# Two transformer blocks in fp32 on one core: weight block sums of the seven-product down projection made on GpSimd

## Chip, cores and metric

One core of one Trainium2 chip runs the whole program. The metric is the device time in microseconds (us). The kernel before was run twice: 1784.21 and 1784.86 us, median 1784.53 us.

## What is computed

Two blocks follow one another on 512 rows of 1024 values: the first holds windowed attention, a gated recurrence and a mixture of experts; the second holds a feed forward layer, a mixer and another feed forward layer. The change lies in the two feed forward layers of the second block.

```python
def swiglu_ffn(x, w_gate, w_up, w_down):
    return (jax.nn.silu(x @ w_gate) * (x @ w_up)) @ w_down

def second_block(x, ...):
    for l in range(DEPTH):
        x = x + 0.5 * swiglu_ffn(rmsnorm(x, ffn1_norm[l]), ffn1_w_gate[l], ffn1_w_up[l], ffn1_w_down[l])
        x = x + hybrid_mixer(rmsnorm(x, mix_norm[l]), w_in[l], ...)
        x = x + 0.5 * swiglu_ffn(rmsnorm(x, ffn2_norm[l]), ffn2_w_gate[l], ffn2_w_up[l], ffn2_w_down[l])
        x = rmsnorm(x, final_norm[l])
    return x
```

The inner width `D_FF` is 2816, and everything is float32.

## The kernel before

Every large product is made of three fp32r products. A weight block of 128x2048 values ("unit") is loaded by a DMA of SyncE's queue into one of four buffers `raw`. ScalarE rounds it into `hi` (`rounded`, line 1862), VectorE makes the rest `lo = raw - hi` (`rest`, line 2271), and TensorE multiplies hi by the high part of the left side, lo by the high part, and hi by the low part. There are two pairs of hi and lo, used in turn: `rounded` of a unit waits until the product that used the pair two units earlier is done. TensorE waits for a unit's hi and lo before its first matmul.

The inner width is worked in three parts (`FPARTS`): 1024, 1024 and 768 columns. For each part come the gate and up products (`mm`, lines 1557 to 1559: a unit serves four blocks of 128 rows, 48 matmuls), then that part's share of the down product. For the first two parts this share is made by a seven-product scheme (a 2 by 2 block product with seven block products in place of eight). `make_plan_ffn` and `schedule_seven` set it out. The down weights of the part are four blocks b11, b21, b12, b22. Four sums of them are made first:

- T3 = b22 - b12, written over b12
- T2 = T3 + b11, written into a buffer of its own, `XW`
- T4 = b21 - T2, written over b21
- T1 = b22 - T2, written over b11

The seven products (`seven`, lines 1526 to 1528, 24 matmuls each) run in this order of weight units: b11, b21, T2, T3, T4, then half of the next part's first gate product, T1, the other half, b22. Their left sides are blocks of the hidden values and sums of them (S1 to S4, A22), whose low parts VectorE makes in `sum_lo` (line 2345). `seven_x` (line 2378) adds each result from PSUM to `x_sb` on VectorE.

So the scheme runs at four places of the program: twice in the first feed forward layer (about 960 and 1085 us) and twice in the second (about 1492 and 1617 us). I call them the four places, and the products by their position, first to seventh.

The order of the work on each engine is one list of steps, written out by hand (`schedule_ffn`, `schedule_seven`); each engine walks the list and does its own kinds of step, in the list's order, and waits on semaphores for the others. In this list T3 and T2 stand inside the up product before the scheme, T4 behind the second product's steps, T1 behind the results of the second and fourth product. The loads stand in the order b12, b22, b11, b21, and each waits until its buffer has been rounded and subtracted (`raw_free`).

GpSimd issues a few small DMAs and makes one addition (line 1364, for the mixer's bias) in this half of the program.

```python
SEVEN = ("P1", "P2", "P6", "P7", "P4", "P5", "P3")
...
            b12, b22 = units(key, wd, r // 128, r // 128 + 8, 512, 1024)
            t1, t2, t4 = (Unit(key, None, 4, 512) for _ in range(3))
...
            plan.extend([b11, b21, t2, b12, t4, g0, t1, g1, b22])
            loads.extend([b12, b22, b11, b21, g0, g1])
```

Of the kernel before, what the change touches and what calls it, by code (L numbers as in the profile page):

```python
# [5 lines left out]
ALU = mybir.AluOpType  # L6
# [845 lines left out]
def program(nc, I, out):  # L852
# [15 lines left out]
    with ctx:  # L868
        sigs = []

        def sig(name, by=1):
            s = Sig(ctx.enter_context(nc.semaphore(name)), by)
            sigs.append(s)
            return s
# [22 lines left out]
        def cst(n):  # L897
            o, w = CW[n]
            return C1[:, o:o + w]

        def bc(a, axis, shape):
            return a.unsqueeze(axis).broadcast_to(shape)
# [141 lines left out]
        d_w = [sig(f"d_w{i}", 16) for i in range(NU)]  # L1044
# [5 lines left out]
        a_hi, v_lo = sig("a_rounded"), sig("v_rest")  # L1050
        p_mm, a_ev, v_ev = sig("p_product"), sig("a_evicted"), sig("v_evicted")
        p_at, a_at, v_at = sig("p_attn"), sig("a_attn"), sig("v_attn")
        p_hg, a_hg, v_hg, g_hg = sig("p_hgrn"), sig("a_hgrn"), sig("v_hgrn"), sig("g_hgrn")
        p_rt, a_rt, v_rt, g_rt = sig("p_route"), sig("a_route"), sig("v_route"), sig("g_route")
        a_sum, v_sum, v_made = sig("a_sum"), sig("v_sum"), sig("v_made")
        p_m2, a_m2, v_m2, g_m2 = sig("p_mix2"), sig("a_mix2"), sig("v_mix2"), sig("g_mix2")

        class Moe:
# [9 lines left out]
        U = p1 + p2 + p3 + p4 + p5  # L1068
# [4 lines left out]
        def split_events(u):  # L1073
            return [(a_hi, u), (v_lo, u)]

        made = {}
# [4 lines left out]
        def blocks(n, p):  # L1081

            return [U.index(q) for q in U if q.key == (n, "s", p)]

        def raw_done(q):

            n, _, p = q.key if q.key[1:2] == ("s",) else (None, None, None)
            u = U.index(q)
            if n and u == blocks(n, p)[0]:
                return split_events(made[n, p, "T1"])  # L1090
            if n and u == blocks(n, p)[1]:
                return split_events(made[n, p, "T4"])
            return split_events(u)

        def place_ffn(first, n, loads, at_raw, at_hl, own=()):
# [81 lines left out]
        n = next(j for j, q in enumerate(experts) if q[:3] == ("gu", "g", NP - 3))  # L1177
        experts, experts_tail = experts[:n], experts[n:]
        experts_tail.insert(1 + next(j for j, q in enumerate(experts_tail) if q[:2] == ("turn_h", NP - 1)), ("table",))
        n, done = schedule_opening(joint, feed3, experts_tail)  # L1180
# [3 lines left out]
        n = after.index(("mm", ("ffn1", "u", 0, 0), 0, 1, first3 + 2))  # L1184
# [138 lines left out]
        def pool_program(pool):  # L1323
            e = pool.e
            def z_load(c):
                pool.wait_ge(d_z[0], (10, 14)[c])
                pool.wait_ge(d_z[1], (11, 15)[c])
                if c == 0:
                    pool.wait_ge(p_mm, (("zb1",), 1, 3))
                else:  # L1330
                    pool.wait_ge(v_hg, ("hTl", 3))
                for w in range(2):
                    e.dma_start(zw[c][w][:, :, :], zsp[8 * w + 4 * c:8 * w + 4 * c + 4, :, :].rearrange("i p n -> p i n")).then_inc(*d_zr[2 * c + w](c))

            def r_load():
                pool.wait_ge(v_hg, ("hTl", 3))
                e.dma_start(n2p[:, :], I["norm2_w"].rearrange("o (p k) -> p (o k)", k=8)).then_inc(*d_r(0))
                e.dma_start(WR[:, :, :], I["w_router"]).then_inc(*d_r(1))
                e.dma_start(BR[:, :], I["b_router"].partition_broadcast(128)[:, 0, :]).then_inc(*d_r(2))

            todo = {"z_load": z_load, "r_load": r_load}
            for name, *a in before + experts:
                if name in todo:
                    todo[name](*a)
            yield None, {}

            def row(name):
                e.dma_start(rows[name][:, :], I[{"ffn1": "ffn1_norm_2", "n2": "mix_norm_2", "ffn2": "ffn2_norm_2"}[name]].partition_broadcast(
                    128)[:, 0, :]).then_inc(*d_row[name](0))

            pool.wait_ge(main.p, ("cols", NP // GP - 1, 7))
            row("ffn1")
            pool.wait_ge(p_mm, (("ffn1", "g", 0, 0), 1, 3))
            row("n2")
            for w, name in enumerate(("q_norm_2", "k_norm_2")):
                for h in range(2):
                    e.dma_start(qkw[64 * h:64 * h + 64, w:w + 1], I[name].rearrange("o d -> d o")).then_inc(*d_b((w, h)))
            e.dma_start(PW[:, :, :], I["pool_w_2"][0].rearrange("g c d -> c g d")).then_inc(*d_b("pool"))

            def m2_bias():  # L1360
                pool.wait_ge(v_norm, ("n2", "l", 3, 1))
                e.dma_start(Bt[:, :, :], I["rel_tile"]).then_inc(*d_bt(0))
                pool.wait_ge(d_bt, 0)
                e.tensor_tensor(Bt[:, :, 128:256], Bt[:, :, 128:256], bc(cst("cmask"), 1, [128, 8, 128]),
                                ALU.add).then_inc(*g_m2("bias"))
                pool.wait_ge(v_ev, (("ffn1", "d", 2, 1), 3))
                e.memset(up[:, :, 0:16], 0.0).then_inc(*g_m2("up0"))

            def m2_row():
                pool.wait_ge(v_m2, ("dd", 3))  # L1370
                row("ffn2")

            todo = {"m2_bias": m2_bias, "m2_row": m2_row}
            for name, *a in after:
                if name in todo:
                    todo[name](*a)
# [472 lines left out]
        def act_program(act):  # L1849
            e = act.e  # L1850

            def rounded(u, part=None):
                q = U[u]
                w = q.kc * q.n
                a, b = ((0, w) if part is None else (part * w // 2, part * w // 2 + w // 2))
                if q.made:
                    act.wait_ge(v_made, (q.made, q.key[0], q.key[2]))
                else:
                    act.wait_ge(d_w[q.slot], u)
                for s, k in q.hl_free:  # L1860
                    act.wait_ge(s, k)
                e.copy(q.hi[:, a:b], q.raw[:, a:b]).then_inc(*a_hi((u, 0) if part == 0 else u))  # L1862
# [250 lines left out]
            def route():  # L2113
# [5 lines left out]
            todo = {"warm": warm_up, "norm": norm, "turned": turned, "rope": rope, "bounds": bounds, "ev": ev, "at_square": at_square, "at_qT": at_qT,  # L2119
                    "at_kT": at_kT, "at_scores": at_scores, "at_turn": at_turn, "at_values": at_values,  # L2120
                    "hg_log": hg_log, "hg_k": hg_k, "z_sig": z_sig, "hg_table": hg_table, "hg_decay": hg_decay, "hg_tail1": hg_tail1, "at_high": at_high,
                    "hg_tail3": hg_tail3, "hg_out": hg_out, "hg_var": hg_var, "hg_turn": hg_turn, "hn": norm_hn,
                    "hn_turn": hn_turn, "hn_half": hn_half, "hnh": hn_high, "route": route}
# [136 lines left out]
        def dve_program(dve):  # L2260
            e = dve.e
# [77 lines left out]
            def sum_lo(n, p, w):  # L2339
# [3 lines left out]
                else:  # L2343
                    dve.wait_ge(a_sum, (w, n, p))
                e.tensor_tensor(l[:, :, :], v, h.bitcast(F32) if w == "A22" else h[:, :, :].bitcast(F32),
                                ALU.subtract).then_inc(*v_sum((w + "l", n, p)))

            def made_(n, p, w):
                b11, b21, t2, b12, t4, t1, b22 = (U[u].raw[:, :] for u in blocks(n, p))
                u11, u21, _, u12, _, u1, u22 = blocks(n, p)  # L2350
                done = v_made((w, n, p))
                if w == "T3":
                    dve.wait_ge(d_w[U[u12].slot], u12)
                    dve.wait_ge(d_w[U[u22].slot], u22)
                    e.tensor_tensor(b12, b22, b12, ALU.subtract).then_inc(*done)
                elif w == "T2":
                    dve.wait_ge(d_w[U[u11].slot], u11)
                    dve.wait_ge(v_made, ("T3", n, p))
                    if p:
                        dve.wait_ge(v_lo, made[n, p - 1, "T2"])  # L2360
                        dve.wait_ge(v_made, ("T1", n, p - 1))
                    e.tensor_tensor(t2, b12, b11, ALU.add).then_inc(*done)
                elif w == "T1":
                    dve.wait_ge(v_lo, u11)
                    dve.wait_ge(v_made, ("T2", n, p))
                    e.tensor_tensor(t1, b22, t2, ALU.subtract).then_inc(*done)
                else:
                    dve.wait_ge(v_lo, u21)
                    dve.wait_ge(v_made, ("T2", n, p))
                    e.tensor_tensor(t4, b21, t2, ALU.subtract).then_inc(*done)  # L2370

            def seven_x(n, p, pr, t):
                r, c = QUARTER[pr]
# [542 lines left out]
            def wo2(tb, c, half):  # L2916
                if half:
# [1 line left out]
                    dve.wait_ge(p_m2, ("wo2", tb, c, 1))  # L2919
                    e.tensor_tensor(v, v, PS[:, c, :], ALU.add).then_inc(*v_m2(("x", tb, c)))  # L2920

            todo = {"sum": sum_, "sum_lo": sum_lo, "made": made_, "seven_x": seven_x, "half": half, "normed": normed, "turned": turned, "turn_hidden": turn_hidden, "ev": ev, "m2_norm": m2_norm, "m2_pool": m2_pool, "m2_scores": m2_scores, "m2_weights": m2_weights,
                    "m2_values": m2_values, "m2_pooled": m2_pooled, "wo2": wo2, "lo": todo["lo"]}
            for name, *a in after:
                if name in todo:
# [170 lines left out]
```

## Time and profile before

| | us |
|---|---|
| the two runs, median | 1784.53 |
| span of the profiled execution | 1785.5 |
| TensorE busy | 1748.2 |
| VectorE busy | 923.1 |
| ScalarE busy | 603.3 |
| GpSimd busy | 12.5 |

The profiled execution is known by its span, 1785.5 us; no separate device time is given for it. The span lies 1.0 us above the median of the runs.

PE is TensorE's matmuls, PEld its weight loads (one goes ahead of each matmul), DVE VectorE, ACT ScalarE, POOL GpSimd, SPq SyncE's DMA queue. In a row of instructions stand the start, the duration, the engine, the line of the kernel, the operation, what it writes and reads, and in brackets how long the engine was idle before it and who released it. Matmuls are pipelined: each is shown as some 390 ns long while one starts every 227 ns.

### The profile page before, as it was taken

The numbers are of one execution on the slowest core, as the hardware profiler recorded it, in microseconds if no ns is written. First come the engines' busy times: TensorE is split into PE (matmuls) and PEld (weight loads), VectorE is DVE, ScalarE is ACT, GpSimd is POOL, SyncE is SP. The second block draws the span as 40 slices with busy tenths as digits, with TensorE's granted clock in tenths as the row PEclk, the third lists the DMA queues.
The fourth block names the chain that finished last, engine by engine and source line by source line (L and its number), as shares of the span: only waits on it lengthen the run. The fifth ranks groups of instructions, "written<-read, shape, count | busy, mean of one in ns | idle before, by whom it ended". The sixth has DMA issues, their size and how long they took to land.

```text
span 1785.5 us, 20614 instructions
## 1 busy us (share of the span) xinstructions
PE 1748.2 (98%) x8607; PEld 1284.3 (72%) x8607; DVE 923.1 (52%) x1339; ACT 603.3 (34%) x938; POOL 12.5 (1%) x22
## 2 busy tenths in 40 slices
PE   7999999998999999999999999999999999999998
PEld 6878888875454544544478888888877888888886
DVE  5768865643333333333444745635578535736634
ACT  4556335442111111111233323324355433423322
POOL 0000000000000000000000000000000000000000
PEclk9999999998999999999999999999999999999999
DMA  6222225547999999999832242233321232241331
GB/s 219 90 71 72 95 83 177 192 161 288 422 421 421 421 421 421 420 421 421 340 114 71 72 141 71 91 122 98 115 71 37 80 133 71 71 159 54 108 104 59
DMA packets 93315, 331.16 MB, mean 185 GB/s; under 512 B 6192, under 2 KB 15552, under 8 KB 68512
## 3 DMA queue, kind: packets, MB, share of 16 engines
q1 hardware_dynamic: 88928, 318.33, 46.8%
q0 software_dynamic: 1984, 7.25, 1.2%
q10 hardware_dynamic: 2304, 4.20, 0.6%
q8 instruction: 70, 1.15, 0.3%
q14 instruction: 29, 0.24, 0.0%
HBM read 323.46 MB, written 6.29 MB: 185 GB/s over the span
## 4 chain that ended last, share of the span: by engine, by line
PE 91%; DVE 5%; ACT 3%; DMA 0%; issue 0%; SPq 0%; DVEq 0%; ACTq 0%
PE PS L1427 12%; PE PS L1557 11%; PE PS L1559 10%; PE PS L1558 10%; PE PS L1460 6%; PE PS L1553 5%; PE PS L1555 5%; PE PS L1554 5%; PE PS L1527 3%; PE PS L1528 3%; PE PS L1526 3%; PE PS L1398 2%; PE PS L1470 2%; PE PS L1399 2%; PE PS L1631 2%; PE PS L1471 2%
## 5 line engine op out<-in xcount | busy, mean ns | idle before, releaser
L2271 DVE TENSOR_TENSOR lo<-raw,hi 128x1024 fp32r<-128x1024 f32 (+2 forms) x147 | 250.4, 1709 | 318.7 <-ACT hi L1862 315.5
L1862 ACT CAST hi<-raw 128x1024 fp32r<-128x1024 f32 (+2 forms) x149 | 214.2, 1446 | 297.9 <-PE PS L1559 111.9
L1557 PE MATMUL PS<-xh_ffn,hi 128*128 128x512 f32 x576 | 225.0, 391 | 0.0
L1559 PE MATMUL PS<-xh_ffn,lo 128*128 128x512 f32 x576 | 224.3, 389 | 0.0
L1558 PE MATMUL PS<-xl_ffn,hi 128*128 128x512 f32 x576 | 224.2, 389 | 0.0
L1559 PEld LDWEIGHTS PS<-xh_ffn,lo 128*128 128x128 f32 x576 | 108.1, 188 | 22.6
L1558 PEld LDWEIGHTS PS<-xl_ffn,hi 128*128 128x128 f32 x576 | 108.2, 188 | 22.2
L1557 PEld LDWEIGHTS PS<-xh_ffn,hi 128*128 128x128 f32 x576 | 108.2, 188 | 22.2
L1427 PE MATMUL PS<-raw,XG 128*64 128x512 f32 x352 | 117.1, 593 | 0.0
L2231 DVE TENSOR_TENSOR HF<-SG,PS 128x512 f32<-128x512 f32 x16 | 17.4, 1090 | 165.0 <-PE PS L1427 165.0
L2246 DVE SCALAR_TENSOR_TENSOR YL<-PS,SM,YH 128x512 fp32r<-128x512 f32 x30 | 21.1, 746 | 138.8 <-ACT YH L1845 138.8
L2254 DVE TENSOR_TENSOR x_sb<-x_sb,PS 128x512 f32<-128x512 f32 x128 | 78.2, 677 | 8.7 <-PE PS L1471 8.7
L1557 PE MATMUL PS<-xTh,hi 128*128 128x512 f32 x192 | 78.3, 408 | 0.5 <-DVE lo L2271 0.3
L1427 PE MATMUL PS<-rawz,XG 128*64 128x512 f32 x280 | 77.7, 592 | 0.0
L1559 PE MATMUL PS<-xTh,lo 128*128 128x512 f32 x192 | 75.0, 391 | 0.0
L1558 PE MATMUL PS<-xTl,hi 128*128 128x512 f32 x192 | 75.0, 391 | 0.0
L1427 PEld LDWEIGHTS PS<-raw,XG 128*64 128x64 f32 x352 | 36.4, 137 | 49.6 <-issue 49.5
L1828 ACT COPY HT<-PS 128x512 f32<-128x512 f32 x16 | 9.4, 586 | 175.1 <-PE PS L1436 175.1
L1398 PE MATMUL PS<-SE,hnh 128*128 128x256 f32 x256 | 65.4, 294 | 0.2 <-DVE SE L2204 0.2
L1399 PE MATMUL PS<-SE,hnl 128*128 128x256 f32 x256 | 63.7, 288 | 0.0
L1427 PEld LDWEIGHTS PS<-rawz,XG 128*64 128x64 f32 x280 | 24.8, 137 | 38.8 <-issue 38.8
L1845 ACT ACTIVATE YH<-PS,SM 128x512 fp32r<-128x512 f32 x30 | 19.0, 683 | 99.8 <-PE PS L1460 99.8
(510 smaller groups left out, 3678.3 us busy)
## 6 DMA issues: line engine op xcount, KB each, us to landing
raw<-in_w_in SPq DMA_DIRECT2D x26, 1024.0 KB, 5.2
rawz<-in_w_down_experts SPq DMA_DIRECT2D x25, 1024.0 KB, 10.1
raw<-in_w_up_experts SPq DMA_DIRECT2D x24, 1024.0 KB, 14.8
raw<-in_w_gate_experts SPq DMA_DIRECT2D x20, 1024.0 KB, 15.0
raw<-in_ffn_w_down SPq DMA_DIRECT2D x20, 1024.0 KB, 5.0
rawz<-in_w_up_experts SPq DMA_DIRECT2D x19, 1024.0 KB, 18.8
raw<-in_w_down_experts SPq DMA_DIRECT2D x16, 1024.0 KB, 11.5
rawz<-in_w_gate_experts SPq DMA_DIRECT2D x16, 1024.0 KB, 13.1
```

The costliest lines, as they stand in the source:

```text
L1398: e.matmul(PS[:, b, 0:GP * 128], hnh[:, tb, f], sv, start=tb == 0, stop=False)
L1399: x = e.matmul(PS[:, b, 0:GP * 128], hnl[:, tb, f], sv, start=False, stop=tb == 3)
L1427: x = e.matmul(PS[64 * q:64 * q + 64, b, :], XG[(i // GP) % 2][:, k, s:s + 64], w[q][:, kk * 512:kk * 512 + 512], start=k == 0, stop=k == 7)
L1460: x = e.matmul(PS[64 * q:64 * q + 64, b + c, :], HT[:, j, 64 * q:64 * q + 64], w[q][:, jj * D + c * 512:jj * D + c * 512 + 512], start=j = ...
L1553: e.matmul(o, xh[:, k, c], h[:, kk, :], start=s0, stop=False)
L1554: e.matmul(o, xh[:, k, c], l[:, kk, :], start=False, stop=False)
L1555: x = e.matmul(o, xl[:, k, c], h[:, kk, :], start=False, stop=s1)
L1557: e.matmul(o, h[:, kk, c], xh[:, k, :], start=s0, stop=False)
L1558: e.matmul(o, h[:, kk, c], xl[:, k, :], start=False, stop=False)
L1559: x = e.matmul(o, l[:, kk, c], xh[:, k, :], start=False, stop=s1)
L1862: e.copy(q.hi[:, a:b], q.raw[:, a:b]).then_inc(*a_hi((u, 0) if part == 0 else u))
L2271: e.tensor_tensor(q.lo[:, a:b], q.raw[:, a:b], q.hi[:, a:b].bitcast(F32), ALU.subtract).then_inc(*v_lo(key))
```

## The change

The four sums of blocks are made by GpSimd, with the same operations and operands. They signal `g_made` in place of `v_made`. Waits that VectorE's own order made needless are written out: T2 waits for the up product's first eviction (its buffer XW is in use before), and the buffer of T3 is reloaded only after T2 has read it. Nothing else on any engine is changed.

```diff
@@ raw_done, inside program
                 return split_events(made[n, p, "T4"])
+            if q.made == "T3":
+                return split_events(u) + [(g_made, ("T2", n, p))]
             return split_events(u)
@@ pool_program
-            todo = {"m2_bias": m2_bias, "m2_row": m2_row}
+            def made_(n, p, w):
+                b11, b21, t2, b12, t4, t1, b22 = (U[u].raw[:, :] for u in blocks(n, p))
+                u11, u21, _, u12, _, u1, u22 = blocks(n, p)
+                done = g_made((w, n, p))
+                if w == "T3":
+                    pool.wait_ge(d_w[U[u12].slot], u12)
+                    pool.wait_ge(d_w[U[u22].slot], u22)
+                    e.tensor_tensor(b12, b22, b12, ALU.subtract).then_inc(*done)
+                elif w == "T2":
+                    pool.wait_ge(d_w[U[u11].slot], u11)
+                    pool.wait_ge(g_made, ("T3", n, p))
+                    if p:
+                        pool.wait_ge(v_lo, made[n, p - 1, "T2"])
+                        pool.wait_ge(g_made, ("T1", n, p - 1))
+                    else:
+                        pool.wait_ge(v_ev, ((n, "u", 0, 0), 3))
+                    e.tensor_tensor(t2, b12, b11, ALU.add).then_inc(*done)
+                elif w == "T1":
+                    pool.wait_ge(v_lo, u11)
+                    pool.wait_ge(g_made, ("T2", n, p))
+                    e.tensor_tensor(t1, b22, t2, ALU.subtract).then_inc(*done)
+                else:
+                    pool.wait_ge(v_lo, u21)
+                    pool.wait_ge(g_made, ("T2", n, p))
+                    e.tensor_tensor(t4, b21, t2, ALU.subtract).then_inc(*done)
+
+            todo = {"m2_bias": m2_bias, "m2_row": m2_row, "made": made_}
@@ rounded, in act_program
-                    act.wait_ge(v_made, (q.made, q.key[0], q.key[2]))
+                    act.wait_ge(g_made, (q.made, q.key[0], q.key[2]))
@@ dve_program
-            def made_(n, p, w):
...
```

VectorE's instructions at the first place, from the rest of b21 (raw_52) to the rest of T4, before. XW is T2, raw_49 holds T3, raw_51 b11 and raw_50 b22:

```order
L2271 TENSOR_TENSOR lo_56<-raw_52,hi_54 128x1024 [waits a_rounded] x2
L2345 TENSOR_TENSOR S2l<-hA,S2h 128x1024 [waits a_sum]
L2378 SCALAR_TENSOR_TENSOR x_sb<-PS,x_sb 128x512 [waits p_product] x2
L2271 TENSOR_TENSOR lo_55<-XW,hi_53 128x2048 [waits a_rounded]
L2370 TENSOR_TENSOR raw_52<-raw_52,XW 128x2048 [waits v_made,v_rest]
L2271 TENSOR_TENSOR lo_56<-raw_49,hi_54 128x2048 [waits a_rounded]
```

The same stretch of VectorE after the change:

```order
L2299 TENSOR_TENSOR lo_56<-raw_52,hi_54 128x1024 [waits a_rounded] x2
L2373 TENSOR_TENSOR S2l<-hA,S2h 128x1024 [waits a_sum]
L2382 SCALAR_TENSOR_TENSOR x_sb<-PS,x_sb 128x512 [waits p_product] x2
L2299 TENSOR_TENSOR lo_55<-XW,hi_53 128x2048 [waits a_rounded]
L2299 TENSOR_TENSOR lo_56<-raw_49,hi_54 128x2048 [waits a_rounded]
```

T4 is gone from between the rests of T2 and T3; T1, which stood eight rows further on, is gone as well. GpSimd's instructions between its small DMAs and the mixer's bias, after the change (before, the bias DMA of line 1362 followed the small DMAs at once):

```order
L1382 TENSOR_TENSOR raw_49<-raw_50,raw_49 128x2048 [waits d_w4,d_w3]
L1391 TENSOR_TENSOR XW<-raw_49,raw_51 128x2048 [waits v_evicted,g_made,d_w5]
L1399 TENSOR_TENSOR raw_52<-raw_52,XW 128x2048 [waits g_made,v_rest]
L1395 TENSOR_TENSOR raw_51<-raw_50,XW 128x2048
L1382 TENSOR_TENSOR raw_49<-raw_52,raw_49 128x2048 [waits d_w0,d_w3]
```

These are T3, T2, T4 and T1 of the first place, then T3 of the second. T3 waits for its two loads alone, T4 for the rest of b21, and T1 has no wait left: it stands directly behind T4.

## Rows read from the trace of the kernel before

**Rows 1.** The page: span, busy time, chain that ended last.

```profile
span 1785.5 us, 20614 instructions
...
PE 1748.2 (98%) x8607; PEld 1284.3 (72%) x8607; DVE 923.1 (52%) x1339; ACT 603.3 (34%) x938; POOL 12.5 (1%) x22
...
PE 91%; DVE 5%; ACT 3%; DMA 0%; issue 0%; SPq 0%; DVEq 0%; ACTq 0%
```

**Rows 2.** Four places by stage: stretch, length, busy by engine, PEclk, DMA, GB/s.

```profile
960.00:1030.00 70.00, 70.00 (x311) 57.99 (x310) 50.43 (x48) 25.23 (x20) 0.00 (x0) 1.00 0.20 64
1085.00:1155.00 70.00, 70.00 (x310) 58.00 (x309) 51.17 (x48) 25.10 (x21) 0.00 (x0) 1.00 0.16 51
1492.00:1562.00 70.00, 70.00 (x311) 57.96 (x310) 50.16 (x48) 25.50 (x20) 0.00 (x0) 1.00 0.20 65
1617.00:1687.00 70.00, 70.00 (x310) 57.98 (x309) 51.23 (x49) 25.36 (x21) 0.00 (x0) 1.00 0.16 52
```

**Rows 3.** Lines 2355, 2362, 2366: duration ns min/median/max, first and last start us.

```profile
L2355 DVE TENSOR_TENSOR raw<-raw,raw x4: 2282/2283/2284, 967.0 to 1624.3; 128x2048 f32<-128x2048 f32 x4
...
L2362 DVE TENSOR_TENSOR XW<-raw,raw x4: 2292/2292/2294, 969.3 to 1626.7; 128x2048 f32<-128x2048 f32 x4
...
L2366 DVE TENSOR_TENSOR raw<-raw,XW x4: 2282/2283/2284, 1010.0 to 1666.7; 128x2048 f32<-128x2048 f32 x4
```

**Rows 4.** Timeline, VectorE, first place: start, duration, instruction, idle before.

```profile
986.40 2.36 DVE L2271 TENSOR_TENSOR lo<-raw,hi 128x1024 fp32r<-128x1024 f32 x2 [0.39 <-ACT hi L1862]
988.68 1.22 DVE L2345 TENSOR_TENSOR S2l<-hA,S2h 128x1024 fp32r<-128x1024 f32 x1
989.82 1.28 DVE L2378 SCALAR_TENSOR_TENSOR x_sb<-PS,x_sb 128x512 f32<-128x512 f32 x2
991.80 2.29 DVE L2271 TENSOR_TENSOR lo<-XW,hi 128x2048 fp32r<-128x2048 f32 x1 [0.70 <-ACT hi L1862]
994.01 2.28 DVE L2370 TENSOR_TENSOR raw<-raw,XW 128x2048 f32<-128x2048 f32 x1
996.91 2.29 DVE L2271 TENSOR_TENSOR lo<-raw,hi 128x2048 fp32r<-128x2048 f32 x1 [0.62 <-ACT hi L1862]
```

**Rows 5.** Line 1526, weight loads: the third, fourth, sixth product; the second place's third.

```profile
L1526 PEld LDWEIGHTS PS<-hi,S2h x8: 188/188/188, 994.5 to 999.3; 128*128 128x128 f32 x8
...
L1526 PEld LDWEIGHTS PS<-hi,S3h x8: 187/188/188, 1000.0 to 1004.7; 128*128 128x128 f32 x8
...
L1526 PEld LDWEIGHTS PS<-hi,S1h x8: 187/188/188, 1021.7 to 1026.5; 128*128 128x128 f32 x8
...
L1526 PEld LDWEIGHTS PS<-hi,S2h x8: 187/188/188, 1119.7 to 1124.4; 128*128 128x128 f32 x8
```

**Rows 6.** Timeline of ScalarE, the roundings at the first place.

```profile
962.81 1.90 ACT L1862 CAST hi<-raw 128x2048 fp32r<-128x2048 f32 x1
973.25 1.91 ACT L1862 CAST hi<-raw 128x2048 fp32r<-128x2048 f32 x1 [8.54 <-PE PS L1559]
...
989.85 1.92 ACT L1862 CAST hi<-XW 128x2048 fp32r<-128x2048 f32 x1 [1.59 <-PE PS L1528]
994.96 1.92 ACT L1862 CAST hi<-raw 128x2048 fp32r<-128x2048 f32 x1 [3.19 <-PE PS L1528]
...
1012.37 1.91 ACT L1862 CAST hi<-raw 128x2048 fp32r<-128x2048 f32 x1 [3.61 <-DVE raw L2366]
```

**Rows 7.** GpSimd's one addition, and VectorE's next instruction after it.

```profile
1266.27 2.40 POOL L1364 TENSOR_TENSOR Bt<-Bt,C 128x1024 f32<-128x1024 f32 x1 [4.67 <-DMA Bt<-in_rel_tile]
...
1269.46 2.29 DVE L2271 TENSOR_TENSOR lo<-raw,hi 128x2048 fp32r<-128x2048 f32 x1 [6.75 <-ACT hi L1862]
```

**Rows 8.** Loads of b22 and b11 as issued, and the loads' time to landing.

```profile
942.97 0.37 SPq L1274 DMA_DIRECT2D raw<-in_ffn_w_down  x1
...
956.18 0.37 SPq L1274 DMA_DIRECT2D raw<-in_ffn_w_down  x1
...
raw<-in_ffn_w_down SPq DMA_DIRECT2D x4, 1024.0 KB, 5.0
```

More of the change, by code:

```diff
@@ L1054, in program @@
         p_rt, a_rt, v_rt, g_rt = sig("p_route"), sig("a_route"), sig("v_route"), sig("g_route")
-        a_sum, v_sum, v_made = sig("a_sum"), sig("v_sum"), sig("v_made")
+        a_sum, v_sum, g_made = sig("a_sum"), sig("v_sum"), sig("g_made")
         p_m2, a_m2, v_m2, g_m2 = sig("p_mix2"), sig("a_mix2"), sig("v_mix2"), sig("g_mix2")
@@ L2346, in sum_lo @@
                                 ALU.subtract).then_inc(*v_sum((w + "l", n, p)))
-            def made_(n, p, w):
[L2349 to L2370, printed above, removed]
             def seven_x(n, p, pr, t):
@@ L2920, in wo2 @@
                     e.tensor_tensor(v, v, PS[:, c, :], ALU.add).then_inc(*v_m2(("x", tb, c)))
-            todo = {"sum": sum_, "sum_lo": sum_lo, "made": made_, "seven_x": seven_x, "half": half, "normed": normed, "turned": turned, "turn_hidden": turn_hidden, "ev": ev, "m2_norm": m2_norm, "m2_pool": m2_pool, "m2_scores": m2_scores, "m2_weights": m2_weights,
+            todo = {"sum": sum_, "sum_lo": sum_lo, "seven_x": seven_x, "half": half, "normed": normed, "turned": turned, "turn_hidden": turn_hidden, "ev": ev, "m2_norm": m2_norm, "m2_pool": m2_pool, "m2_scores": m2_scores, "m2_weights": m2_weights,
                     "m2_values": m2_values, "m2_pooled": m2_pooled, "wo2": wo2, "lo": todo["lo"]}
```

## The prediction

> **What bounds the kernel now.** I read the page first. TensorE is busy for 1748.2 of 1785.5 us and carries 91% of the chain that ended last; VectorE has half its time free and GpSimd nearly all of it [rows 1]. A share over the whole span says little of one stage, so I then cut the four places of the change out, 70 us each. In every one the matmuls fill 70.00 of 70.00 us at full granted clock, while VectorE is busy for 50 to 51 us and ScalarE for 25 [rows 2]. TensorE never waits there. So nothing that VectorE is spared at these places can shorten the program: its removed time was already hidden. What can change is the other sign. A unit's rest (lo) must be ready before its product starts, and how much time it has to spare decides whether a disturbance is seen.
>
> I read that spare time from the timeline of VectorE at the first place against the weight loads of the products. The rest of T2 starts at 991.80 and takes 2.29 us, so it ends at 994.1 [rows 4]; the third product's first weight load is at 994.5 [rows 5]. 0.4 us to spare. The rest of T3 ends at 996.91 + 2.29 = 999.2, and the fourth product starts at 1000.0: 0.8 us. The reason for so little is that there are only two hi/lo pairs: the rounding of T2 starts when the first product is done (989.85, released by TensorE), the rounding of T3 when the second is (994.96) [rows 6], and one product takes about 5.4 us, while rounding and rest take 1.9 + 2.3 = 4.2. At the second place the third product starts at 1119.7 [rows 5], 125.2 later than at the first, and the pattern is the same; the third and fourth place repeat them.
>
> **The change, part by part.**
>
> *Removed from VectorE:* 16 subtractions and additions of 128x2048, 2.28 to 2.29 us each [rows 3], 36.6 us in all. VectorE falls to about 886 us. Gain on the path: none, by the full TensorE of rows 2. T1 shows this well. ScalarE waits 3.61 us for it before it rounds at 1012.37 [rows 6], which looks like a cost, but the sixth product starts only at 1021.7 [rows 5]. That wait goes and nothing is gained: what ends last there is TensorE's own queue.
>
> *Added to GpSimd:* the same 16 operations. The only two-input operation of GpSimd in the trace is the bias addition, 2.40 us for 1024 elements a partition, with VectorE idle all the while (its next instruction starts at 1269.46) [rows 7]. VectorE takes 1.22 us for 1024 [rows 4] and 2.28 for 2048, so 0.16 us of an operation is fixed. For 2048 elements on GpSimd the bounds are 2.3 us, if it were as quick as VectorE at that length, and 4.8 us, twice the row. I take 4.7, just under twice the row since some part will be fixed as on VectorE. GpSimd's busy time rises from 12.5 to some 88 us. The Trainium skill (GPSIMD Engine Reference, Performance versus the Vector engine) gives 4.5 us for this operation and 2.29 for VectorE's; rows 3 agree with the second, and rows 7 with a ratio of about two.
>
> *T3 and T2.* T3 now needs only its loads. b22 is issued at 942.97 and lands 5.0 later [rows 8], so T3 runs at 948.0 to 952.7. b11 is issued at 956.18, so T2 runs at 961.2 to 965.9. It is wanted at 989.85 [rows 6]: 24 us to spare. Cost nothing, even if GpSimd's first operation starts some microseconds late. If T2 disturbs the rest of an up unit, that costs nothing either: two roundings are there 10.4 us apart (962.81 and 973.25) [rows 6], and rounding, a whole GpSimd operation and the rest take 1.9 + 4.7 + 2.3 = 8.9.
>
> *T4 and T1, as results.* T4 may start when the rest of b21 ends, 986.40 + 2.36 = 988.8 [rows 4], and its rounding waits for the third product's end, about 1000.4 (one product of 5.4 behind 994.96). T1 stands directly behind T4 on GpSimd with no wait of its own, and is wanted at about 1011. Alone they would be done at 993.5 and 998.2. On time.
>
> *T4 and T1, as neighbours.* Here is the cost. Before, no two-input operation ran on both engines at once. Now T4 and T1 fill some 9.4 us just when the rests of T2 and T3, with 0.4 and 0.8 us to spare, must run. No row shows the two engines reading together, so I bound it: below by nothing (they do not disturb each other; a gain is excluded by the full TensorE), above by one operation waiting for the whole of the other. I take the upper end in its plain form, in which the engine that has waited goes first. GpSimd needs 2.34 ns for an element against VectorE's 1.2 [rows 7, 4], as an engine does that fetches its two inputs one after another over one way, so I expect that way to be full and not to leave room for a partner. This is a choice, not a reading.
>
> Step by step: S2l holds until 988.68 + 1.22 = 989.9 [rows 4]. T4 runs 989.9 to 994.6. The additions to x_sb have one input in PSUM and go on. The rest of T2, ready to start at 991.80, waits until 994.6 and ends at 996.9: the third product starts 2.4 us late (994.5 to 996.9). T1 has waited longest and runs 996.9 to 1001.6; the rest of T3 runs 1001.6 to 1003.9, where the fourth product was due at 1000.0 + 2.4 = 1002.4: 1.5 more. Then GpSimd is done, and the rest of T4 has only its usual neighbours. Together 3.9 us a place; with D for the GpSimd operation this is 2D - 5.5. TensorE is full behind, so nothing gives it back. Four places: 4 x 3.9 = 15.6 us, a span of 1785.5 + 15.6 = 1801.1; the span is 1.0 above the median of the runs, so 1784.5 + 15.6 = 1800.1 us, or 0.9% slower.
>
> The Trainium skill speaks against this change (SBUF — State Buffer, Who interferes with whom): a VectorE instruction with both inputs in SBUF fetches the second through the read interface that GpSimd uses, and the same section tells of a lock on the shared ports held for a whole instruction, whoever starts first. By this rule of the Trainium skill, with the 4.5 us of its GPSIMD Engine Reference, the place costs 2 x 4.5 - 5.5 = 3.5 us and the time is 1798.5. The trace of the kernel before neither shows nor denies it.
>
> *The written-out waits:* the wait of T2 for the up eviction is long over, and the reload of T3's buffer waits anyway for T3's own rest, 30 us after T2. Nothing. GpSimd's later work (the bias at 1266 [rows 7]) stands 130 us behind T1 of the second place. Nothing.
>
> **Rivals.**
>
> *The two engines do not disturb each other (not slower).* Then the removed time was hidden, the added time is hidden, and the time stays at 1784.5. For it: nothing in the trace speaks of interference, and one product's spare time is untouched. Against it: only that the operations are of the kind that might share. It decides if the rest of T2 still takes 2.3 us beside T4. A stretch of it by up to 0.4 us is free too.
>
> *They share.* Both slow down while they overlap. An operation of VectorE may then stretch between not at all and, with the whole of GpSimd's 4.7 us added, three times; at some 1.6 times the rest of T2 takes 3.7 us, ends at about 995.5 (S2l before it ends 0.7 later, still in time) and costs 1.0 to 1.1; the rest of T3 ends at 1000.5, in time for 1001.1. 4 x 1.1 = 4.4: 1789 us.
>
> *GpSimd keeps its turn.* T1 has no wait, so it may follow T4 before VectorE gets in. Then the rest of T2 ends at 989.9 + 9.4 + 2.3 = 1001.6, 7.1 late; the rest of T3 ends at 1003.9, before 1007.1. 4 x 7.1 = 28.4: 1812.9 us. It would be slower by over 2% (8.9 us a place) if an operation took over 5.6 us, since the place costs 2D - 2.3.
>
> **How the numbers follow.** Whole operations wait, in turn: 0.47 (1795 to 1801 as one or both rests wait; 1800.1 is the point). Share: 0.20. No disturbance: 0.20. GpSimd keeps its turn: 0.10, of which a third with operations slow enough to pass 2%. Rest 0.03. The range runs from 1783.8, to hold the case without disturbance with the spread of the runs (0.65 us), to 1808, which leaves out the case of the kept turn. A measurement tells about 2% (36 us) from no change: faster 0.01, within 2% 0.95, slower by more 0.04.
>
> **What would show each step.** The profile after should have 16 additions on GpSimd, 4.5 to 4.8 us long where undisturbed; T3 at 948 and T2 at 961; T4 within 1 us of the end of S2l, T1 right behind it or behind one VectorE operation. The waiting shows as a rest of T2 that starts or ends 2 to 3 us late, be it as idle time or as a duration of 5 us, and as waits of line 1526 for line 2299, twice a place, 2.4 and 1.5 us. TensorE busy in the four stretches would fall from 70 to about 66. I am wrong if those rests keep 2.3 us (no disturbance), if they stretch to 3 to 4 us (sharing), or if TensorE waits somewhere else, above all at T3 or T2.

## The result, and the profile after

The changed kernel took 1800.95 and 1803.22 us, median 1802.09, against 1784.53 before: 1.0095 times as long, 95% interval 1.0078 to 1.0112. Forecast were 1800.1 us and a range of 1783.8 to 1808.0. The ratios and intervals here and below are those recorded with the runs; they differ from the quotients of the medians (here 1.0098) by up to 0.0004. The profiled execution's device time was 1800.95 us, its span 1798.8. Measured again in five runs on one chip with the kernel before (e1_after), the ratio is 1.0083 (1.0070 to 1.0097). The cost is well under the 2% that the prediction took as the least that a measurement can tell, and still clear of the scatter.

The page of the kernel after, answering to [rows 1]:

```profile
span 1798.8 us, 20614 instructions
...
PE 1748.6 (97%) x8607; PEld 1281.7 (71%) x8607; DVE 925.9 (51%) x1323; ACT 603.5 (34%) x938; POOL 98.0 (5%) x38
...
PE 89%; DVE 6%; ACT 4%; issue 0%; DMA 0%; SPq 0%; DVEq 0%; ACTq 0%
```

TensorE does the same work in a span 13.3 us longer. The odd number is VectorE's: it lost 36.6 us of work and is shown busier than before, 925.9 against 923.1. So something else is counted as its busy time, and the waiting is not to be looked for under idle time alone.

The four places, by stage, answering to [rows 2]:

```profile
960.00:1030.00 70.00, 66.73 (x294) 54.66 (x293) 48.47 (x43) 23.66 (x19) 16.00 (x3) 1.00 0.19 61
1085.00:1155.00 70.00, 66.73 (x294) 54.65 (x293) 50.56 (x44) 23.78 (x20) 16.76 (x3) 1.00 0.20 64
1492.00:1562.00 70.00, 66.73 (x294) 54.65 (x293) 49.66 (x43) 23.91 (x21) 16.76 (x3) 1.00 0.23 76
1617.00:1687.00 70.00, 66.74 (x294) 54.64 (x293) 50.71 (x41) 24.34 (x21) 21.38 (x4) 1.00 0.17 54
```

TensorE now has the same 3.3 us idle in each. The granted clock stays at 1.00, so the stalls cost their own length and no more. VectorE at the first place, answering to [rows 4]:

```profile
986.66 1.22 DVE L2373 TENSOR_TENSOR S2l<-hA,S2h 128x1024 fp32r<-128x1024 f32 x1
987.79 1.28 DVE L2382 SCALAR_TENSOR_TENSOR x_sb<-PS,x_sb 128x512 f32<-128x512 f32 x2
989.77 4.73 DVE L2299 TENSOR_TENSOR lo<-XW,hi 128x2048 fp32r<-128x2048 f32 x1 [0.70 <-ACT hi L1890]
994.86 6.26 DVE L2299 TENSOR_TENSOR lo<-raw,hi 128x2048 fp32r<-128x2048 f32 x1 [0.36 <-ACT hi L1890]
1001.04 0.68 DVE L2382 SCALAR_TENSOR_TENSOR x_sb<-PS,x_sb 128x512 f32<-128x512 f32 x1
```

GpSimd in the same stretch (T2, T4, T1), in the timeline:

```profile
959.24 4.61 POOL L1391 TENSOR_TENSOR XW<-raw,raw 128x2048 f32<-128x2048 f32 x1 [8.49 <-DMA raw<-in_ffn_w_down]
986.82 5.54 POOL L1399 TENSOR_TENSOR raw<-raw,XW 128x2048 f32<-128x2048 f32 x1 [22.97 <-DVE lo L2299]
992.30 6.67 POOL L1395 TENSOR_TENSOR raw<-raw,XW 128x2048 f32<-128x2048 f32 x1
```

Read the ends, not the starts. A sum takes 4.61 us on GpSimd when alone. T4 is shown from 986.82, but S2l holds until 987.88, and 987.88 + 4.5 is T4's end, 992.36. The rest of T2 is shown as 4.73 us long; it ends at 994.50, 2.1 after T4's end, which is its own 2.29 less 0.15 (rows of VectorE that follow one another overlap by 0.08 or so anyway). T1 is shown as 6.67 us long and ends at 998.97, 4.5 after the rest of T2. The rest of T3, 6.26 us long, ends at 1001.12, 2.15 after T1. Five instructions, each of which runs only when the one before it on the other engine has ended. The additions to x_sb, with one input in PSUM, take 1.28 us in the midst of T4, as before.

TensorE's weight loads in the timeline, and the fourth product's first matmul, show what comes of it:

```profile
994.58 0.19 PEld L1554 LDWEIGHTS PS<-hi,S2h 128*128 128x128 f32 x1 [2.10 <-issue]
...
1001.84 0.19 PEld L1554 LDWEIGHTS PS<-hi,S3h 128*128 128x128 f32 x1 [1.95 <-issue]
```

```profile
1001.87 0.47 PE L1554 MATMUL PS<-hi,S3h 128*128 128x512 f32 x1 [1.56 <-DVE x_sb L2382]
```

The third product starts 0.08 us after the rest of T2 ends (994.50): it waited for that rest, although no releaser is named. The fourth starts 0.72 us after the rest of T3 ends (1001.12), so that rest is not the last thing that it waits for. The row names another: the addition to `x_sb` that stands behind the rest of T3 on VectorE. It ends at 1001.72, and the weight load follows 0.12 later; at the second and third place, and in e4 and e7 below, it follows such an addition by 0.11 to 0.12 as well. The kernel has this wait, in `seven`: from the third product on, a block may begin only when an earlier result has been added from the same PSUM bank (for the fourth product, index 3, that of the third, index 2):

```python
            pe.wait_ge(a_hi, u)
            pe.wait_ge(v_lo, u)
            ...
                pe.wait_ge(v_sum, ("x", n, p, {2: 0, 3: 2, 4: 3, 5: 1, 6: 5}[pr], t))
```

The kernel before has the same addition behind the same rest, ending at 999.80, just ahead of the fourth product's first weight load:

```profile
999.12 0.68 DVE L2378 SCALAR_TENSOR_TENSOR x_sb<-PS,x_sb 128x512 f32<-128x512 f32 x1
```

```profile
999.98 0.19 PEld L1526 LDWEIGHTS PS<-hi,S3h 128*128 128x128 f32 x1
```

So the rest of T3 had not 0.8 us to spare, as the prediction read from the end of the rest, but less than 0.1: 999.98 less 999.80, less the 0.12 from the addition's end to the load.

For the cost of a place I use a distance that one row shows: ScalarE rounds T2 once at each place, and first and last start are three places apart. Line 1862 before and line 1890 after:

```profile
L1862 ACT CAST hi<-XW x4: 1909/1912/1917, 989.9 to 1647.0; 128x2048 fp32r<-128x2048 f32 x4
```

```profile
L1890 ACT CAST hi<-XW x4: 1912/1914/1917, 987.8 to 1656.4; 128x2048 fp32r<-128x2048 f32 x4
```

657.1 us before and 668.6 after: 11.5 / 3 = 3.8 us a place, 15.3 for four. (The distance holds the first three places. Behind the last rounding of T2 the span runs on for 138.5 us before and 142.4 after, 3.9 more: that is the fourth place, and nothing else behind it costs.) The stretch ahead of the first place, which the change does not touch, is 2.0 us shorter in this execution (987.8 against 989.9), which is why the spans differ by 13.3 and not 15.3. Such differences come and go between executions of one kernel (before ranged from 1783.76 to 1787.39 us in 21 runs beside e1) and are not the change's.

### The profile page after: what moved, and what is told of

It reads as the page before. It is cut to its first block, busy times and chain, and to the rows that moved or that the text cites. A ratio compares the mean times of both kernels' runs of the same rounds, so it can differ in the third digit from the quotient of the medians.

```text
span 1798.8 us, 20614 instructions
## 1 busy us (share of the span) xinstructions
PE 1748.6 (97%) x8607; PEld 1281.7 (71%) x8607; DVE 925.9 (51%) x1323; ACT 603.5 (34%) x938; POOL 98.0 (5%) x38
## 4 chain that ended last, share of the span: by engine, by line
PE 89%; DVE 6%; ACT 4%; issue 0%; DMA 0%; SPq 0%; DVEq 0%; ACTq 0%
PE PS L1455 12%; PE PS L1585 10%; PE PS L1587 10%; PE PS L1586 10%; PE PS L1488 6%; PE PS L1581 5%; PE PS L1583 5%; PE PS L1582 5%; PE PS L1554 2%; PE PS L1556 2%; PE PS L1555 2%; DVE lo L2299 2%; PE PS L1426 2%; PE PS L1427 2%; PE PS L1498 2%; PE PS L1659 2%
## 5 line engine op out<-in xcount | busy, mean ns | idle before, releaser
L2299 DVE TENSOR_TENSOR lo<-raw,hi 128x1024 fp32r<-128x1024 f32 (+2 forms) x147 | 278.0, 1896 | 326.1 <-ACT hi L1890 322.8
L1498 PE MATMUL PS<-YH,ST 128*128 128x512 f32 x128 | 52.2, 408 | 0.4 <-DVE YL L2265 0.4
```

The costliest lines, as they stand in the source:

```text
L2299: e.tensor_tensor(q.lo[:, a:b], q.raw[:, a:b], q.hi[:, a:b].bitcast(F32), ALU.subtract).then_inc(*v_lo(key))
```

## The experiments

The theory, from the trace after: a GpSimd instruction that reads SBUF and a VectorE instruction with both inputs in SBUF run in turns, each waiting for the whole of the other. The rivals: both are slowed in proportion while they overlap; the cost is in another part of the change; GpSimd keeps its turn. The kernel before was run beside each group: its medians are 1785.40 us for e1 to e4, 1785.43 for e5 to e8 and 1785.50 for e9 and e10. "Distance" is that from the first to the last rounding of T2, 657.1 us before.

**The changed kernel again, and its two halves.** e1_after is the kernel after without an edit.

> The changed kernel again, against the kernel before on one chip. Theory (turns): a GpSimd subtraction and a VectorE instruction with both inputs in SBUF wait for each other's end, in turn; in the trace after, ScalarE's rounding of T2 stands at 987.83 against 989.85 before and the rounding of b22 at 1029.43 against 1027.65, so one place costs 3.8 us and four cost 15.2: 1.0085 of before. Rival (something beside the four places costs too, since the runs differed by 17.6 us): 1.0095 to 1.011, with a stretch outside the places that is longer in the trace.

1799.73 us, 1.0083 (1.0070 to 1.0097) of before. First to last rounding of T2 668.5 us: 3.8 a place. That is 14.3 us over before. The interval alone does not exclude the rival's 1.0095, but the trace shows no stretch outside the places that is longer: 986.6 us ahead of the first rounding of T2 (989.9 before), and behind the last 142.4 again, with the fourth place in it. The rest of the 17.6 us of the first comparison, two runs against two, did not come back.

In e2 and e3 the sums are shared out; each wait for a sum goes to the engine that makes it. (T2 also waits for T4 of the place before, which is long done.) The edit against the kernel before in short (e3 has `('T4', 'T1')`):

```diff
+        ON_POOL = ('T3', 'T2')
+
+        def by(w):
+            return g_made if w in ON_POOL else v_made
...
-                    act.wait_ge(v_made, (q.made, q.key[0], q.key[2]))
+                    act.wait_ge(by(q.made), (q.made, q.key[0], q.key[2]))
```

> T3 and T2 on GpSimd, T4 and T1 on VectorE as before. Turns: T2 holds one rest of an up unit by 1 us (3.28 in place of 2.29, seen after), which has over 6 us to spare, so the time is that of before within 1 us (0.9995 to 1.0005). Rival (the written-out waits, the later reload of T3's buffer or GpSimd's start cost something): 2 to 5 us more than before.

1785.41 us, ratio 1.0002 (0.9993 to 1.0011), distance 657.1: nothing. The written-out waits and the later reload are free. The two sums do make VectorE wait: at the first and third place one rest of an up unit takes 3.33 us in place of 2.29, and at the second and fourth two do, 4.3 to 5.2 us each, one for T3 and one for T2. All of it stays inside the time that these rests have to spare.

> T4 and T1 on GpSimd, T3 and T2 on VectorE as before. Turns: the whole cost is here, 4 x 3.8 = 15.2 us over before (1.0085), the same as the changed kernel within 1 us. Rival (cost spread over all four sums): 7 to 11 us.

1800.66 us, 1.0085 (1.0071 to 1.0098), distance 668.6: 3.8 a place, the whole cost.

**T4 alone.**

> T4 alone on GpSimd, T3, T2 and T1 on VectorE. Turns: the rest of T2 waits for T4's end (4.7 us long in place of 2.3) and the third product starts 2.0 to 2.4 us late; nothing waits for the rest of T3. Cost 2.2 us a place, 8 to 10 us over before, 1.0045 to 1.0055. Rival (both are slowed in proportion to what overlaps): half of the 3.8 us, 7.6 us over before, with a rest of T2 of 3 to 4 us.

1793.27 us, 1.0046 (1.0032 to 1.0060), distance 663.1: 2.0 us a place. VectorE's and GpSimd's timelines at the first place:

```profile
988.46 4.74 DVE L2307 TENSOR_TENSOR lo<-XW,hi 128x2048 fp32r<-128x2048 f32 x1 [0.70 <-ACT hi L1898]
993.55 2.29 DVE L2307 TENSOR_TENSOR lo<-raw,hi 128x2048 fp32r<-128x2048 f32 x1 [0.35 <-ACT hi L1898]
```

```profile
985.51 5.53 POOL L1407 TENSOR_TENSOR raw<-raw,XW 128x2048 f32<-128x2048 f32 x1 [68.38 <-DVE lo L2307]
```

The time alone does not part the two theories: it is 7.8 us over before, between the 8 to 10 of the one and the 7.6 of the other. The rows do. The rest of T2 takes 4.74 us and not 3 to 4, and the rest of T3 is whole again. And T4 ends at 991.04, 4.5 us after S2l (986.56), as in the changed kernel: the rest that stands ready beside it from 988.46 on does not slow it at all.

**T1 moved behind the rest of T3.**

```diff
                 elif w == "T1":
                     pool.wait_ge(v_lo, u11)
+                    pool.wait_ge(v_lo, u12)
```

> As the changed kernel, but T1 also waits for the rest of T3. Turns: the rest of T2 still waits for T4 (2.2 us), the rest of T3 waits for nobody, T1 runs between it and the rest of T4 and holds A22's rest for 1 to 2 us, with up to 0.5 us seen by TensorE: 2.2 to 2.7 us a place, 9 to 11 us over before. Rival (the cost goes with GpSimd's busy time beside VectorE, wherever it stands): 15 us over before as in the changed kernel.

1797.55 us, 1.0068 (1.0054 to 1.0082), distance 666.1: 3.0 us a place, 12.1 us over before. Less than 3.8 (and than the rival's 15 us), more than the 2.2 to 2.7 expected. The timelines of VectorE, GpSimd and the weight loads show where I was off:

```profile
993.58 2.29 DVE L2300 TENSOR_TENSOR lo<-raw,hi 128x2048 fp32r<-128x2048 f32 x1 [0.35 <-ACT hi L1891]
996.37 0.69 DVE L2383 SCALAR_TENSOR_TENSOR x_sb<-PS,x_sb 128x512 f32<-128x512 f32 x1 [0.50 <-PE PS L1557]
996.98 4.67 DVE L2374 TENSOR_TENSOR A2ll<-SG,A2h 128x1024 fp32r<-128x1024 f32 x1
1001.57 0.68 DVE L2383 SCALAR_TENSOR_TENSOR x_sb<-PS,x_sb 128x512 f32<-128x512 f32 x1
1002.17 2.27 DVE L2300 TENSOR_TENSOR lo<-raw,hi 128x2048 fp32r<-128x2048 f32 x1
```

```profile
995.95 4.62 POOL L1396 TENSOR_TENSOR raw<-raw,XW 128x2048 f32<-128x2048 f32 x1 [4.87 <-DVE lo L2300]
```

```profile
1002.30 0.19 PEld L1555 LDWEIGHTS PS<-hi,S3h 128*128 128x128 f32 x1 [0.95 <-DVE x_sb L2383]
```

The rest of T3 takes 2.29 us as expected. But the rest of A22 comes 1.0 us after T1's start and waits for its end at 1000.57: 3.5 us, where I had put 1 to 2. Behind it on VectorE stands the addition to `x_sb` for which the second half of the fourth product waits. It ends at 1002.25, and the weight load follows at 1002.30; with 0.2 more at the fifth product, which waits for the next such addition, that is the 1.0 us over T4 alone. A wait in turns is paid by whoever comes next in the engine's order, even where the instruction that waits is not itself urgent.

**T4 and T1 in pieces.** Four subtractions of 512 columns, or eight of 256:

```diff
+            def pieces(o, a, b, done):
+                for k in range(0, 2048, 512):
+                    x = e.tensor_tensor(o[:, k:k + 512], a[:, k:k + 512], b[:, k:k + 512], ALU.subtract)
+                x.then_inc(*done)
...
-                    e.tensor_tensor(t1, b22, t2, ALU.subtract).then_inc(*done)
+                    pieces(t1, b22, t2, done)
```

> As the changed kernel, but T4 and T1 are each four GpSimd subtractions of 128x512 in place of one of 128x2048. Turns: a piece takes about 1.2 us, so a rest waits for at most one piece; of that 0.4 us (T2) and 0.8 us (T3) are spare, and the place costs 0 to 1.2 us in place of 3.8: 0 to 5 us over before, 1.000 to 1.003. Rival (GpSimd keeps its turn over its own pieces): the rest of T2 waits for all four or eight pieces, 15 to 28 us over before. Rival (both are slowed all the while they overlap): the overlap is as long as it was, so 10 to 15 us over before.

1788.85 us, 1.0023 (1.0014 to 1.0032), distance 660.2: 1.0 us a place, inside what was expected (0 to 1.2). The rests of T2 and T3 at the first place, in the timeline:

```profile
988.84 2.67 DVE L2304 TENSOR_TENSOR lo<-XW,hi 128x2048 fp32r<-128x2048 f32 x1 [0.70 <-ACT hi L1895]
993.95 3.37 DVE L2304 TENSOR_TENSOR lo<-raw,hi 128x2048 fp32r<-128x2048 f32 x1 [2.44 <-ACT hi L1895]
```

They wait 0.4 and 1.1 us, at most one piece (1.29 us alone), although six more stand behind that piece on GpSimd in the first case and three in the second: it does not keep its turn. The wait of 0.4 is inside the spare time of T2; of the 1.1 nearly all is seen, since the addition to `x_sb` behind the rest of T3 had under 0.1 us to spare.

> As the changed kernel, with T4 and T1 each in eight GpSimd subtractions of 128x256, some 0.6 us each. Turns: a VectorE instruction waits for at most one piece; a place costs 0 to 0.6 us in place of 1.0 with pieces of 512 and 3.8 with 2048: 0 to 2.5 us over before. Rival (slowed all the while they overlap, and the pieces of 512 only made the overlap looser): no better than the pieces of 512, 3.5 to 5 us over before.

1786.67 us, 1.0007 (0.9998 to 1.0016), distance 657.9: 0.3 us a place by the distance; the interval of the times reaches 1. All four sums are still made by GpSimd here, and T4 and T1 take longer than whole (pieces and waits run on for 19.4 us at the first place, against 12.2 for the two whole sums). Were the slowing in proportion to the overlap, this would be the dearest version.

**Does it take reading?** GpSimd fills the buffers of T4 and T1 twice over in place of the subtractions; T4 and T1 are not computed.

```diff
+            def written(o, w, n, p, done):
+                e.memset(o, 0.5).then_inc(*done)
+                pool.wait_ge(g_made, (w, "first", n, p))
+                e.memset(o, 0.5).then_inc(*g_made((w, n, p)))
```

> T4 and T1 are not computed: GpSimd fills their buffers twice with a constant, at the same place of the program, which reads nothing from SBUF. Theory (it is reading that the two engines do in turns): the rests of T2 and T3 keep 2.29 us, and the time is that of before within 1.5 us. Rival (any GpSimd instruction on SBUF makes a two-input VectorE instruction wait): the rests of T2 and T3 are longer by up to one fill, and the time is 4 us or more over before.

1785.80 us, 1.0003 (0.9994 to 1.0012), distance 657.2. GpSimd's second and third fill, and the rest of T2 on VectorE beside them, in the timelines:

```profile
987.66 1.82 POOL L1378 MEMSET raw<- 128x2048 f32 x1
989.43 1.81 POOL L1376 MEMSET raw<- 128x2048 f32 x1
```

```profile
988.77 2.29 DVE L2304 TENSOR_TENSOR lo<-XW,hi 128x2048 fp32r<-128x2048 f32 x1 [0.70 <-ACT hi L1895]
```

None is longer than without a neighbour (2.29 and 1.81 us, to 0.01), here and at the other three places. (The fills are over when the rest of T3 begins at 993.87, so only the rest of T2 tests the rule.) In e9 GpSimd copies one block in place of each subtraction of two (T4 and T1 are again not computed):

```diff
-                    e.tensor_tensor(t1, b22, t2, ALU.subtract).then_inc(*done)
+                    e.tensor_copy(t1, b22).then_inc(*done)
...
-                    e.tensor_tensor(t4, b21, t2, ALU.subtract).then_inc(*done)
+                    e.tensor_copy(t4, t2).then_inc(*done)
```

> T4 and T1 are not computed: GpSimd copies one 128x2048 block into each buffer, which reads one input of SBUF in place of two. Theory (any GpSimd instruction that reads SBUF takes turns with a two-input VectorE instruction): the rests of T2 and T3 wait for the end of the copy in flight; the copy is shorter than 4.6 us, so the place costs over 0.3 us and less than 3.8, and GpSimd's copies are longer than alone where they meet VectorE. Rival (two inputs on GpSimd's side are needed): rests of 2.29 us and the time of before within 1.5 us.

1787.11 us, 1.0010 (1.0000 to 1.0020), 1.6 us over before, just past the rival's 1.5, distance 658.3. The theory had asked for more than 0.3 us at every place. The time does not decide between them; the rows do, and they differ from place to place. GpSimd's two copies and VectorE's rest of T2, at the first place and then at the second:

```profile
987.32 2.83 POOL L1399 COPY raw<-XW 128x2048 f32<-128x2048 f32 x1 [22.82 <-DVE lo L2299]
990.09 1.90 POOL L1395 COPY raw<-raw 128x2048 f32<-128x2048 f32 x1
...
1113.55 2.83 POOL L1399 COPY raw<-XW 128x2048 f32<-128x2048 f32 x1 [21.35 <-DVE lo L2299]
1116.32 3.97 POOL L1395 COPY raw<-raw 128x2048 f32<-128x2048 f32 x1
```

```profile
990.29 3.84 DVE L2299 TENSOR_TENSOR lo<-XW,hi 128x2048 fp32r<-128x2048 f32 x1 [0.70 <-ACT hi L1890]
...
1116.23 2.29 DVE L2299 TENSOR_TENSOR lo<-XW,hi 128x2048 fp32r<-128x2048 f32 x1 [0.42 <-ACT hi L1890]
```

At the first place the copy starts 0.20 us ahead of the rest: the rest takes 3.84 and the place costs 1.1. At the second the rest starts 0.09 us ahead, keeps its 2.29, and the copy is the one of 3.97; that place and the two after cost nothing. One input read on GpSimd's side is enough, and who starts first has the turn. I had expected a wait at every place and for the rest of T3 too: the copies are over before that rest begins, and it keeps its 2.29 us. The four places are not quite alike either: with the kernel before the rest of T2 follows the start of the second product by 2.7 us at the first place and by 2.4 at the others, which is what lets it win there.

**What the spared work was worth.** In the kernel before, T3, T4 and T1 are cut to 8 columns on VectorE (the rest of them is not computed):

```diff
-                    e.tensor_tensor(b12, b22, b12, ALU.subtract).then_inc(*done)
+                    e.tensor_tensor(b12[:, 0:8], b22[:, 0:8], b12[:, 0:8], ALU.subtract).then_inc(*done)
```

> The kernel before with T3, T4 and T1 cut to 8 of 2048 columns on VectorE (the rest of these sums is not computed), which spares VectorE 12 x 2.2 = 26 us. Theory (the removed work was hidden behind a full TensorE): the time of before within 1.5 us. Rival (VectorE's load in the four places is worth something): 3 us or more faster than before.

1785.44 us, 1.0004 (0.9995 to 1.0014), distance 657.1. VectorE is busy for 898.5 us instead of 923.1, and nothing comes of it.

## Why the prediction was right

- *No gain:* right. Leaving three of the four sums out gains nothing, so a cheaper way to make them cannot gain either.
- *T3 and T2 free:* right, shown by e2. T2 did hold the rest of an up unit for 1 us (3.28 in place of 2.29), inside its 6 us of spare time. At the second and fourth place T3 held one as well, and the waits were 2.0 to 2.9 us long; the prediction allowed for a whole GpSimd operation, and nothing was seen of them in the time.
- *4.7 us for a sum on GpSimd:* 4.61 alone, and 4.5 from release to end where it has waited.
- *One operation waits for the whole of the other, in turn:* this was the choice between far bounds, and it holds. The third product was forecast 2.4 us late and was about 2.1 (994.58, against 994.5 less the 2.0 by which this execution was ahead), the fourth 1.5 more and was 1.7. Together 3.8 a place where 3.9 was forecast, 15.3 in all for 15.6. That the sum comes so close is in part luck. Two sums of 4.5 in place of 4.7 and two rests of 2.14 in place of 2.3 make the chain 0.8 us shorter than forecast: the rest of T3 ends at 1003.1 (1001.12 and the 2.0) where 1003.9 was forecast. But the fourth product does not start there.
- *A term left out:* the addition to `x_sb` behind the rest of T3. The prediction gave the fourth product 0.8 us to spare by the end of that rest; it waits for the addition too, 0.60 us later, with 0.12 to the weight load. This adds 0.7 us a place and nearly cancels the 0.8. Without it the measured durations would give 3.1 to 3.2 us a place.
- *Where it would show:* I left open whether as idle time or as duration. It is duration, on both engines. The waits of the products for line 2299, which I named as a sign, are not listed as such: the third product's has no releaser, and the fourth's is the addition (line 2382).
- *TensorE from 70 to about 66 in a stretch:* 66.7. The matmuls' modelled ends cover some 0.16 us of each of the two stalls, and the first matmul behind each is shown 0.08 longer (0.47 us), so idle time (3.3) is less than the cost (3.8).
- *The rivals:* no disturbance falls by e1 and e3; sharing falls by the ends of the instructions (T4 as long as ever beside a waiting rest, e5) and by e7; the kept turn falls by the trace after (the rest of T2 went in between T4 and T1) and by e4.

The rule of the Trainium skill that I set against the change (SBUF — State Buffer, Who interferes with whom) is borne out: two-input VectorE instructions and reading GpSimd instructions block one another, write-only ones do not, and a VectorE instruction with one SBUF input passes freely (here the additions to `x_sb`, whose other input is in PSUM: 1.28 us for two in the midst of T4). With the 4.5 us of the Trainium skill's GPSIMD Engine Reference (Performance versus the Vector engine) it gave 3.5 us a place; measured are 3.8. The 4.5 us agree with the 4.5 from release to end; what the sum lacks is the addition behind the rest of T3.

What was not tried is a version that makes the changed kernel faster than before; with TensorE full in the four places I would expect nothing there for it to gain. Nor was the addition to `x_sb` moved ahead of the rest of T3, which might give back some of the 0.7 us; no run shows it.

## What to carry to other kernels

Before work goes from VectorE to GpSimd, look for two-input VectorE instructions in SBUF that must end on time near where GpSimd will read: each can come late by up to a whole GpSimd instruction less its spare time, here 4.6 less 0.4 (2.1 us in fact, since T4 was under way). Read the spare time to the end of everything that the consumer waits for and that stands behind in the same engine's order, not to the end of the instruction that is held: here that was an addition that frees a PSUM bank. If the work must go there, cut GpSimd's instructions small (2048, 512 and 256 columns cost 3.8, 1.0 and 0.3 us a place) or put them where nothing urgent stands, as T3 and T2 were. And read first whether the work to be taken away is on the path at all: an engine that is full over the whole stretch says it is not.

## What the runs showed of the hardware

The waiting is in the durations of both engines: an instruction that waits for the other engine is shown as running (VectorE 2.29 us up to 6.27, GpSimd 4.61 up to 6.67), and VectorE looked busier for having less to do. The turn goes to whoever starts first, by as little as 0.1 to 0.2 us, so that the same code cost 1.1 us at the first place and nothing at the other three, where the rest came 0.3 us earlier (e9). And GpSimd's first sum of the program took 4.62 us like the others; nothing of a late start was seen.
